# Decode layer with a mixture of experts: the last chunk's results are added in PSUM instead of stored, and the stored results are requested behind the last weights

## The chip, the cores and the metric

The kernel runs on one core of a Trainium2 chip. The metric is the device time of one execution in microseconds, the median of the runs.

## What is computed

One layer of a decoder for 256 prompt tokens and 32 sample tokens (8 sequences of 4), width 1024, in float32: a token mixer (sparse attention in three branches beside a gated linear recurrence), then a mixture of experts. Only the second half bears on the change:

```python
def moe_ffn(h, w_router, b_router, w_up, b_up, w_down, b_down):
    xt = h.reshape(-1, D)
    top_v, top_i = lax.top_k(xt @ w_router + b_router, TOP_K)      # 4 of 32 experts
    wts = jax.nn.softmax(top_v, axis=-1)
    gate_dense = sum over k of one_hot(top_i, 32) * wts            # token x expert
    for e in range(N_EXPERTS):
        z = xt @ w_up[e] + b_up[e]
        gate, up = min(z[:, :1024], 7), clip(z[:, 1024:], -7, 7)
        act = (up + 1.0) * gate * sigmoid(1.702 * gate)
        out = out + gate_dense[:, e:e + 1] * (act @ w_down[e] + b_down[e])
    return out
```

The layer's result is `x + gate * rms_norm(out)`, for the prompt and for the sample tokens.

## The kernel before

The five engines' programs are written out by hand in one block and meet in counted semaphores. `after(engine, name)` waits for a named step; the steps of TensorE, ScalarE and VectorE are counted in the order of the table `STEPS`. `link` makes an engine wait for its own last instruction.

**Order of the work.** Page gathers, modulation and input projection; attention of the sample tokens; then the prompt phase, in which `prompt_steps()` (a planner with costs in microseconds) lays out attention units (12 of them: two token tiles, three branches, two groups), the recurrence and the branch gates. The gates' weights come in 512 KB pieces into two buffers (`load_gate`, L621); SP asks for piece j once TensorE has used piece j-2 (`gate_ps`), and L1175 multiplies each in two halves. Semaphore `p_pv` counts finished attention units (L1099). Then the projections (L1254 to L1268), the router, and the routing: L2194 to L2234 on VectorE compute each token's row in its expert's chunks, the table `tab` (cumulated chunk counts per expert) and the weights `wts`.

**The expert loop.** The tokens of an expert are cut into chunks of 64 slots (`SLOT`). TensorE loops over experts and their chunks (34 chunks here). For a chunk it multiplies by 8 pieces of `w_up` (L1333), gathers the next chunk's tokens by a product with a 0/1 matrix (`dispatch`, L1304), transposes, and multiplies by 4 pieces of `w_down` into bank 4 (L1363). With 64 slots the two halves of the columns go to partitions 0 to 63 and 64 to 127 of a bank. Each piece of weights is 1 MB; SP issues them in order into a ring of 21 places (`load_piece`, L678), each when its place has been used (`piece_used`). ScalarE copies bank 4 to `yc` (L1715) and GpSimd stores `yc` with an indirect DMA (L2320) to `slots` in device memory, by token and choice, behind a small write (L2319); both count on `st_yc`. VectorE's `rowu` holds the rows.

**The tail.** Behind the weights SP waits for the last use by the last expert but one, then asks for `x` (`xl`, L707, L708), the experts' output bias `bdown` (L709) and the output gates (`gate_last`, L639, L640). Then it waits for `all_out`, which ScalarE gives when the last store has landed (L1718, L1719), and asks for the results of the 32 sample tokens (four loads, L714) and of the two prompt tiles (two loads of 2 MB, L716) into `gath`. TensorE transposes the token-by-expert weights `dense` (L1369; ScalarE copies them to `wT`), starts the sums of all three token tiles with the bias products (L1376), adds the sample rows' results by `wdiag` (L1380) and two of the four results of each prompt tile by `diag` (L1387). ScalarE and VectorE take the sample rows first (`ORDER` is 2, 0, 1): squares, root, `residual`; then `weighted(0)` and `weighted(1)` add the other two results (L2271, L2274), and two `residual` calls follow (L2154, L2156). SP stores y.

The ring, `xl`, `gate_last`, `bdown` and `gath` share one region: `gath` lies on ring places that the last expert still uses.

## Time and profile before

| | |
|---|---|
| median of 3 runs | 1582.41 us (1581.9 to 1583.75) |
| profiled execution | 1583.75 us, its span 1581.7 us |
| TensorE busy | 1450.6 us (92%) |
| VectorE, ScalarE, GpSimd busy | 367.3, 297.3, 81.6 us |
| granted TensorE clock | 0.965 of full speed in the mean |
| DMA | 513.21 MB, 324 GB/s in the mean |
| last request of the tail's first loads, first request of results | 1534.45 us, 1552.12 us |

The span runs from the first to the last instruction; times in the rows are microseconds from its start. An engine is called idle between its instructions, with what released it; a "form" is partitions by elements. The page cuts the span into 40 slices of 39.5 us.

### The profile page before, as it was taken

The page shows a single profiled execution, that of the slowest core. Times are in us where ns is not written, and L with a number is a line of the kernel's source. Part 1 is how long each engine was busy: PE and PEld are TensorE (multiplying, and loading weights), DVE is VectorE, ACT ScalarE, POOL GpSimd, SP SyncE. Part 2 cuts the span into 40 slices and gives each one's busy share as a digit, 9 for nine tenths or more (in the row PEclk, how much of TensorE's full clock was granted, in tenths as well). Part 3 has the DMA queues.
Part 4 walks back from the last instruction along what each step waited for, and adds up shares of the span by engine and source line. Part 5 has one row for each costly group of instructions (what it writes and reads, how often), then busy time and mean ns, then how long its engine had stood idle before and what let it go on. Part 6 is the DMA issues. An engine that isn't in the chain of part 4 may idle for free.

```text
span 1581.7 us, 21206 instructions
## 1 busy us (share of the span) xinstructions
PE 1450.6 (92%) x8595; PEld 649.6 (41%) x8595; DVE 367.3 (23%) x845; ACT 297.3 (19%) x568; POOL 81.6 (5%) x108
## 2 busy tenths in 40 slices
PE   4999989889998969999999999999998998899896
PEld 4554455378876543333333333333332222222221
DVE  5210012346852351111111111010101101110123
ACT  4100004544530221111111111111110110011011
POOL 2000002100000000000000000000000000000000
PEclk9999999978999969999999999999999999999997
DMA  9792774314269589979999999999999999999994
GB/s 276 245 321 80 290 257 171 84 42 140 60 164 292 213 327 383 416 310 417 418 414 417 417 415 416 419 416 415 417 417 417 415 417 417 414 418 416 415 404 175
DMA packets 136310, 513.21 MB, mean 324 GB/s; under 512 B 12945, under 2 KB 42025, under 8 KB 100962
## 3 DMA queue, kind: packets, MB, share of 16 engines
q1 hardware_dynamic: 129474, 489.91, 79.3%
q0 software_dynamic: 6752, 22.06, 4.1%
q8 instruction: 67, 1.10, 0.3%
q14 instruction: 17, 0.14, 0.0%
HBM read 501.06 MB, written 19.22 MB: 329 GB/s over the span
## 4 chain that ended last, share of the span: by engine, by line
PE 60%; DMA 29%; DVE 5%; SPq 3%; ACT 2%; issue 1%; POOL 0%; DVEq 0%; POOLq 0%; ACTq 0%
DMA arena<-in_w_up 23%; PE bank L1333 20%; PE bank L1363 9%; PE bank L1175 4%; PE bank L783 3%; PE bank L999 3%; PE bank L1000 3%; DMA arena<-in_w_in 2%; SPq L678 2%; PE bank L1268 2%; DMA arena<-in_cache_cmp,arena 2%; PE bank L1325 1%; PE bank L1254 1%; PE bank L1073 1%; PE bank L1256 1%
## 5 line engine op out<-in xcount | busy, mean ns | idle before, releaser
L1333 PE MATMUL bank<-arena 128*64 128x512 f32 x2176 | 498.0, 600 | 36.6 <-DMA arena<-in_w_up 36.3
L1333 PEld LDWEIGHTS bank<-arena 128*64 128x64 f32 x2176 | 145.0, 137 | 359.5 <-issue 262.0
L1363 PE MATMUL bank<-arena 128*64 128x512 f32 x1088 | 241.0, 595 | 0.0
L2245 DVE TENSOR_SCALAR arena<-bank,arena 128x1 uint32<-128x1 f32 x34 | 7.4, 219 | 597.7 <-PE bank L1341 580.4
L1363 PEld LDWEIGHTS bank<-arena 128*64 128x64 f32 x1088 | 75.0, 136 | 141.7 <-issue 135.7
L1708 ACT ACTIVATE arena<-arena 128x512 f32<-128x512 f32 x34 | 21.4, 630 | 536.3 <-DVE arena L2248 536.3
L1304 PE MATMUL bank<-arena 128*64 128x512 f32 (+1 forms) x420 | 103.0, 608 | 2.9 <-DVE arena L2206 2.9
L2319 POOL DMA_DIRECT2D slots<-arena x34 | 18.7, 551 | 1188.3 <-ACT arena L1715 1188.3
L1175 PE MATMUL bank<-arena 128*128 128x288 f32 x256 | 75.5, 445 | 2.4 <-DMA arena<-in_w_in 1.5
L2248 DVE TENSOR_SCALAR arena<-bank 128x512 f32<-128x512 f32 x34 | 23.5, 692 | 190.4 <-PE bank L1333 190.4
L999 PE MATMUL bank<-arena 128*128 128x512 f32 (+1 forms) x112 | 57.0, 590 | 8.4 <-DMA arena<-in_w_in 6.8
L1715 ACT COPY arena<-bank 128x512 f32<-128x512 f32 x34 | 19.9, 586 | 221.5 <-PE bank L1363 221.5
L1175 PEld LDWEIGHTS bank<-arena 128*128 128x128 f32 x256 | 51.3, 209 | 19.0 <-issue 2.8
L1304 PEld LDWEIGHTS bank<-arena 128*64 128x64 f32 (+1 forms) x420 | 26.9, 135 | 72.5 <-issue 69.4
L783 PE MATMUL bank<-arena 64*128 64x504 f32 x256 | 54.7, 584 | 1.7 <-DVE arena L1775 1.7
L1000 PE MATMUL bank<-arena 128*128 128x512 f32 (+1 forms) x112 | 55.9, 581 | 0.0
L1708 ACT ACT_TABLE_LOAD x34 | 43.6, 1283 | 0.6
L1325 PE MATMUL bank<-arena 32*64 32x512 f32 x272 | 37.9, 626 | 1.2 <-ACT arena L1699 1.2
L783 PEld LDWEIGHTS bank<-arena 64*128 64x128 f32 x256 | 25.1, 186 | 30.3 <-issue 30.3
L761 PE MATMUL bank<-arena 128*128 128x128 f32 x128 | 20.9, 325 | 17.1 <-DMA arena<-in_cache_cmp,arena 16.2
L2320 POOL DMA_INDIRECT slots<-arena x34 | 35.5, 1044 | 10.4 <-issue 10.4
L999 PEld LDWEIGHTS bank<-arena 128*128 128x128 f32 x112 | 21.5, 197 | 32.1 <-issue 22.4
(418 smaller groups left out, 1298.8 us busy)
## 6 DMA issues: line engine op xcount, KB each, us to landing
arena<-in_w_up SPq DMA_DIRECT2D x256, 1024.0 KB, 20.9
arena<-in_w_down SPq DMA_DIRECT2D x128, 1024.0 KB, 25.0
arena<-in_w_ada SPq DMA_DIRECT2D x12, 2048.0 KB, 11.8
arena<-in_w_in SPq DMA_DIRECT2D x6, 2048.0 KB, 13.2
arena<-in_w_in SPq DMA_DIRECT2D x16, 512.0 KB, 4.1
arena<-in_w_out SPq DMA_DIRECT2D x1, 4096.0 KB, 16.6
arena<-slots SPq DMA_DIRECT2D x2, 2048.0 KB, 10.3
out<-in_state_win SPq DMA_DIRECT2D x1, 4064.0 KB
```

Source lines behind the costliest of these rows:

```text
L678: sp.dma_start(dst, src).then_inc(S(f"ld_piece{n % R_}"), 16)
L783: last = mm(banks[2 * g + v][:, 0:NB * NCMP], w1[half, s], src, start=s == 0, stop=s == 31)
L999: mm(b0[:, 0:w], hT[:, k, 0:P], columns(k, 0, w), start=first, stop=final)
L1000: mm(b1[:, 0:w], hT[:, k, P:2 * P], columns(k, 0, w), start=first, stop=final)
L1175: last = mm(banks[7][:, 0:TP + NS], gate_piece[j % 2][:, k], hT[:, k], start=k == 0, stop=k == KD - 1)
L1268: last = mm(banks[(6, 2)[i] + n][:], mT[:, k, P * i:P * i + P], wo[k][:, 512 * n:512 * n + 512], start=k == 0, stop=k == KD - 1)
L1304: last = mm(banks[5][SLOT * s:SLOT * s + SLOT, :], oneslot[0:ROWS[i], i], h2r[0:ROWS[i], i, 512 * s:512 * s + 512], start=i == 0, stop=i == 2)
L1325: mm(banks[r // 2][SLOT * (r % 2):SLOT * (r % 2) + SLOT, :], ident[32 * r:32 * r + E, 32 * r + e:32 * r + e + 1].broadcast_to([E, SLOT]), ...
L1333: last = mm(banks[part][SLOT * s:SLOT * s + SLOT, :], xcT[:, q], ring[n % R_][:, D * part + 512 * s:D * part + 512 * s + 512], start=False ...
L1363: last = mm(banks[4][SLOT * s:SLOT * s + SLOT, :], lhs, ring[n % R_][:, D * v + 512 * s:D * v + 512 * s + 512], start=f == 0, stop=f == 7)
L1708: fn(sg, gt, ACT.Sigmoid, scale=1.702).then_inc(S("sig"), 1)
L2320: pool.indirect_dma_start(out=results, out_offset=bass.IndirectOffsetOnAxis(ap=rowu[:, 0:1], axis=0), in_=yc, in_offset=None, bounds_check ...
```

## The change

The last chunk is no longer stored. ScalarE still copies its result to `yc`; TensorE adds it to the three sums by products with `lastT`, a matrix slot by token that holds the token's weight where the token has that slot in the last chunk. So:

- GpSimd's loop runs over all chunks but the last. Rows of `slots` that the last chunk would have filled must be zero: early in the kernel GpSimd zeroes all of `slots` (4.72 MB, from a 128x128 tile of zeros, once the sixth attention unit is through) and waits for it.
- SP waits only for the stores of the chunks before the last (`st_yc` at `until * 32`) and asks for the results straight behind the gates.
- The output bias is loaded twice, to partitions 0 to 31 and 32 to 63, and the weights by expert are laid out twice (`dense2`), so that the two column halves of a bias product use different rows of the array. In the same way `lastT` holds the slots twice, beside the two halves of `yc`.
- VectorE computes the last chunk's first row (`last_row`), each token's weight in it (`last_k`, `last_sum`) and its slot (`slot0`) in the routing, builds `dense2` and `last_w` after its loop, and copies the transposed `lastT` out of bank 7 ahead of the diagonals.
- `gath` moves down by one ring place, to places that the last expert does not use.

```diff
@@ sync
-            sp.dma_start(bdown[0:E], A["b_down"][0]).then_inc(S("ld_bias"), 16)
+            for v in range(2):
+                sp.dma_start(bdown[E * v:E * v + E], A["b_down"][0]).then_inc(S("ld_bias"), 16)
             broadcast_rows(gate_last, 3 * D, "ld_gate")
-            after(sp, "all_out")
+            until = sp.value_load(tab[0:1, 3 * E - 1:3 * E], min_val=E - 1, max_val=CMAX - 1)
+            sp.wait_ge(S("st_yc"), until * 32)
@@ tensor
-            after(pe, "wdiag")
+            after(pe, "last_w")
             for i in range(3):
-                last = nc.tensor.transpose(banks[5][0:E, P * i:P * i + ROWS[i]], dense[0:ROWS[i], i], ident[0:ROWS[i], 0:ROWS[i]])
+                last = nc.tensor.transpose(banks[5][0:2 * E, P * i:P * i + ROWS[i]], dense2[0:ROWS[i], i], ident[0:ROWS[i], 0:ROWS[i]])
             last.then_inc(S("wT_ps"), 1)
+            for i in range(3):
+                last = nc.tensor.transpose(banks[7][:, P * i:P * i + ROWS[i]], last_w[0:ROWS[i], i], ident[0:ROWS[i], 0:ROWS[i]])
+            last.then_inc(S("lastT_ps"), 1)
             after(pe, "wT")
-            pe.wait_ge(S("ld_bias"), 80)
+            pe.wait_ge(S("ld_bias"), 96)
...
+            def down_bias(i):
                 for v in range(2):
+                    mm(banks[summed_in[i][v]][0:ROWS[i], :], wT[E * v:E * v + E, P * i:P * i + ROWS[i]],
+                       bdown[E * v:E * v + E, 512 * v:512 * v + 512], start=True, stop=False)
+
+            def last_rows(i):
+                for v in range(2):
+                    mm(banks[summed_in[i][v]][0:ROWS[i], :], lastT[SLOT * v:SLOT * v + SLOT, P * i:P * i + ROWS[i]],
+                       yc[SLOT * v:SLOT * v + SLOT, :], start=False, stop=False)
+
+            down_bias(0)
+            down_bias(1)
+            after(pe, "lastT")
+            down_bias(2)
+            after(pe, "yc_last")
+            for i in ORDER:
+                last_rows(i)
             pe.wait_ge(S("ld_gath2"), 64)
@@ scalar
-            act.wait_ge(S("st_yc"), n_chunks * 32)
-            nc.scalar.copy(gathered, eps_t).then_inc(S("all_out"), 1)
+            act.wait_ge(S("yc"), n_chunks)
+            nc.scalar.copy(gathered, eps_t).then_inc(S("yc_last"), 1)
@@ vector
+            V.memset(zero_t, 0.0).then_inc(S("zero_t"), 1)
...
             after(dve, "base_ps")
+            V.tensor_scalar(last_row, banks[3][:, 5 * E - 1:5 * E], float(SLOT), float(-SLOT), ALU.mult, ALU.add)
...
             V.tensor_scalar(wdiag, C("stack32"), wst, None, ALU.mult).then_inc(S("wdiag"), 1)
+            for i in range(3):
+                r = ROWS[i]
+                last = V.scalar_tensor_tensor(last_k[0:r, 4 * i:4 * i + 4], rowf[0:r, 4 * i:4 * i + 4], last_row[0:r], wts[0:r, i],
+                                              ALU.is_ge, ALU.mult)
+            link(dve, "dve", last)
+            for i in range(3):
+                last = V.tensor_reduce(last_sum[0:ROWS[i], i:i + 1], last_k[0:ROWS[i], 4 * i:4 * i + 4], AX, ALU.add)
+            link(dve, "dve", last)
+            until = dve.value_load(tab[0:1, 3 * E - 1:3 * E], min_val=E - 1, max_val=CMAX - 1)
+            V.tensor_copy(slot0, slot_of[:, :, bass.ds(until, 1)].rearrange("p i o -> p (i o)"))
+            link(dve, "dve", V.tensor_copy(ss[:, 3:4], eps_t))
...
+            for v in range(2):
+                V.tensor_copy(dense2[:, 0:2, E * v:E * v + E], dense[:, 0:2])
+                V.tensor_copy(dense2[0:NS, 2, E * v:E * v + E], dense[0:NS, 2])
+            for i in range(3):
+                for v in range(2):
+                    last = V.tensor_scalar(last_w[0:ROWS[i], i, SLOT * v:SLOT * v + SLOT], C("slot1")[0:ROWS[i]], slot0[0:ROWS[i], i:i + 1],
+                                           last_sum[0:ROWS[i], i:i + 1], ALU.is_equal, ALU.mult)
+            last.then_inc(S("last_w"), 1)
+            after(dve, "lastT_ps")
+            V.tensor_copy(lastT[:, 0:TP + NS], banks[7][:, 0:TP + NS]).then_inc(S("lastT"), 1)
@@ gpsimd
+            after(pool, "zero_t")
+            rows = slots[0:NRES].rearrange("(p a) (b c) -> p (a b) c", p=P, c=P)
+            pool.wait_ge(S("p_pv"), 6)
+            pool.dma_start(rows, zero_t.unsqueeze(1).broadcast_to([P, rows.shape[1], P])).then_inc(S("zero_slots"), 16)
+            pool.wait_ge(S("zero_slots"), 16)
             after(pool, "tab")
-            n_chunks = pool.value_load(tab[0:1, E - 1:E], min_val=E, max_val=CMAX)
-            with pool.Fori(0, n_chunks) as c:
+            until = pool.value_load(tab[0:1, 3 * E - 1:3 * E], min_val=E - 1, max_val=CMAX - 1)
+            with pool.Fori(0, until) as c:
```

## Rows read from the trace of the kernel before

**Rows 1.** The page: GB/s moved in each of 40 slices.
```profile
GB/s 276 245 321 80 290 257 171 84 42 140 60 164 292 213 327 383 416 310 417 418 414 417 417 415 416 419 416 415 417 417 417 415 417 417 414 418 416 415 404 175
```

**Rows 2.** Chain that ended last, the tail: start, length, what.
```profile
1547.33 0.59 ACT arena L1715
...
1549.44 2.44 DMA slots<-arena
...
1554.33 12.48 DMA arena<-slots
...
1566.86 3.71 PE bank L1387 x8
...
1572.04 1.28 DVE arena L2274
...
1577.41 1.23 DVE arena L2156
```

**Rows 3.** Windows: length, PE, PEld, DVE, ACT, POOL busy, PEclk, DMA share, GB/s.
```profile
1540.00:1545.00 5.00, 5.00 (x26) 1.75 (x26) 1.04 (x5) 0.59 (x1) 0.00 (x0) 1.00 0.77 264
1545.00:1550.00 5.00, 4.41 (x19) 1.51 (x16) 0.00 (x0) 0.87 (x2) 1.11 (x2) 0.98 0.15 55
1550.00:1555.00 5.00, 5.00 (x7) 1.35 (x6) 0.00 (x0) 0.19 (x1) 0.48 (x1) 0.50 0.42 127
1555.00:1560.00 5.00, 5.00 (x7) 0.71 (x5) 0.00 (x0) 0.00 (x0) 0.00 (x0) 0.50 1.00 376
1560.00:1565.00 5.00, 3.53 (x9) 1.44 (x8) 1.58 (x4) 2.83 (x6) 0.00 (x0) 0.99 1.00 429
```

**Rows 4.** Timeline of the tail: start, length, engine, line, form, idle before.
```profile
1544.89 0.14 PEld L1363 LDWEIGHTS bank<-arena 128*64 128x64 f32 x2 [0.29 <-DMA arena<-in_w_down]
...
1548.24 9.21 PE L1376 MATMUL bank<-arena 32*128 32x512 f32 x12 [0.59 <-ACT arena L1717]
...
1557.38 3.22 PE L1380 MATMUL bank<-arena 128*32 128x512 f32 x4
...
1560.64 0.59 ACT L1725 ACTIVATE arena<-bank 32x512 f32<-32x512 f32 x1 [8.55 <-PE bank L1380]
...
1563.53 0.15 DVE L2141 RECIPROCAL arena<-arena 32x1 f32<-32x1 f32 x1 [1.36 <-ACT arena L1668]
...
1566.29 1.39 DVE L2271 SCALAR_TENSOR_TENSOR arena<-arena,bank 128x512 f32<-128x512 f32 x2
```

**Rows 5.** SP's requests, and DMA issues of 1526 to 1536 (KB, us to landing).
```profile
1530.60 3.34 SPq L709 DMA_DIRECT2D arena<-in_b_down  x1
...
1534.45 0.76 SPq L640 DMA_DIRECT2D arena<-modd  x1
...
arena<-in_b_down SPq DMA_DIRECT2D x1, 128.0 KB, 17.2
arena<-modd SPq DMA_DIRECT2D x1, 128.0 KB, 14.9
```

**Rows 6.** The page's groups: count, busy us, mean ns, idle before.
```profile
L783 PE MATMUL bank<-arena 64*128 64x504 f32 x256 | 54.7, 584 | 1.7 <-DVE arena L1775 1.7
```

**Rows 7.** The prompt phase: TensorE's timeline, DMA issues of 385 to 395, windows.
```profile
386.12 1.00 PE L1099 MATMUL bank<-arena 128*128 128x64 f32 x8
...
394.61 2.86 PE L1175 MATMUL bank<-arena 128*128 128x288 f32 x8
...
408.05 2.21 PE L1175 MATMUL bank<-arena 128*128 128x288 f32 x8
...
arena<-in_w_in SPq DMA_DIRECT2D x1, 512.0 KB, 15.2
...
390.00:400.00 10.00, 10.00 (x47) 7.93 (x47) 9.14 (x22) 6.89 (x20) 0.00 (x0) 0.83 0.46 184
...
417.00:420.00 3.00, 3.00 (x29) 3.00 (x29) 2.93 (x8) 1.78 (x3) 0.00 (x0) 1.00 0.66 175
```

**Rows 8.** VectorE's timeline, first work of its chunk loop.
```profile
602.67 0.22 DVE L2245 TENSOR_SCALAR arena<-bank,arena 128x1 uint32<-128x1 f32 x1 [6.30 <-PE bank L1341]
```

29 lines of the change are left out of this document (16 added, 13 removed).

## The prediction

> **What bounds the kernel now.** I began with the page's line of bytes per slice [rows 1]. From the nineteenth slice on the DMA engines move 414 to 419 GB/s (404 in the next to last): the expert weights stream at one rate for some 800 us, so work of the expert loop is paid only if it holds that stream back. The last slice shows 175 GB/s: the weights are through and something else sets the end. So the chain that ended last was read next, for the tail only [rows 2]. From the last chunk's result to the end it runs: ScalarE empties bank 4 at 1547.33 (L1715), GpSimd stores the chunk and the store takes 2.44 us to land from 1549.44, SP then issues six loads, the second big load of `slots` lands 12.48 us after 1554.33, TensorE adds its share (3.71 us from 1566.86), and VectorE works to 1578.64 (1577.41 + 1.23). Between there and the span's 1581.7 lies the store of y, 3.06 us.
>
> The windows of that stretch [rows 3] show what is wasted. In 1545 to 1550 the core moves 55 GB/s and in 1550 to 1555 127 GB/s, while nothing but the fetch of results is left to do. The tail waits for bytes that could not be asked for before the last store had landed. The second fact in these windows is the clock: 0.98, 0.50, 0.50, 0.99. TensorE fell to its lower level (1.2 of 2.4 GHz) at about 1549.9, while it ran the bias products of L1376, and came back at about 1560.
>
> The timeline gives the prices [rows 4]. One 128x512 fp32 product shows as two instructions: L1387's eight instructions (four products) take 3.71 us at full clock [rows 2], so one costs some 0.86 us in a longer run. L1376's six products took 9.21 us and L1380's two 3.22, at the lower level. VectorE is nearly back to back once it starts: first reciprocal 1563.53, first weighted sum 1566.29, so the sample rows cost 2.76; a weighted sum costs 2.70 (1.39, 1.28 and the gap); from the end of the second one (1572.04 + 1.28 = 1573.32) to that of the chain [rows 2] are 5.32 for two residuals. ScalarE starts on the sample rows at 1560.64 and VectorE follows 2.89 later.
>
> **Part 1, the loads move forward.** SP's last requests of before end at 1535.21 [rows 5]. The last of them lands 14.9 us after 1534.45, at 1549.35, and the bias 17.2 after 1530.60, at 1547.8: the requests sit in the queue behind the last weights. After the change SP waits only for the next to last chunk's store, which GpSimd issued a chunk earlier (some 30 us), so SP walks through, and the copy of the bias and the results' six loads are asked for from about 1535 to 1539. They land behind 1549.35. Their bytes are 0.13 + 0.52 + 2.10 + 2.10 MB; the fetch ran at 429 GB/s in 1560 to 1565 [rows 3]. That gives the second bias copy about 1548.1 (0.3 behind the first), the sample rows 1550.9, the first prompt tile 1555.8, the second 1560.7. In the kernel before the second landed at 1566.81 (1554.33 + 12.48). I take the slowest DMA engine for this: those that are done early (share 0.77 in 1540 to 1545) only help.
>
> Does this traffic slow the last weights? TensorE took the last `w_down` piece with the same 0.29 us gap as between any two weight loads [rows 4], so there is no slack. Between 0 and +1 us (a gain is excluded: nothing ahead of them is taken away); I take 0, since the requests stand behind the weights in the same queue and the stream shows one rate with all engines busy.
>
> The Trainium skill ("DMA: Bandwidth & Descriptors", Queues, rings and completion order) says that descriptors of one queue start in ring order on each engine. By it this cost is zero too; no row here shows two requests of one queue overtaking, and the sum above does without it.
>
> **Part 2, the last store goes.** It frees 1547.92 to 1552.1 on the chain. ScalarE now signals `yc_last` right behind its copy of the 64 rows of wT, at about 1548.5. No cost.
>
> **Part 3, new products.** TensorE transposes wT (now 64 columns) and then three more tiles: short ones, beside ScalarE's copy of bank 4. VectorE then copies 128x288 out of PSUM ahead of the diagonals, no more than the 0.59 us of ScalarE's 128x512 copy [rows 2]. The bias products of tiles 0 and 1 start when they did, at 1548.24, and cover that copy. Bias products now come in pairs on two 32-row strips and the last chunk's in pairs on two 64-row strips. Pairs of this sort exist in the kernel: L783, on 64 rows, shows 256 instructions in 54.7 us busy [rows 6], 0.214 us each, so a pair (four instructions) costs 0.86 us, what one product alone costs. Three bias pairs: 2.6 us instead of 9.21. Three last-chunk pairs: 2.6 us new. Two sample products: 1.7 us. Sum at full clock: 1548.24 + 2.6 + 2.6 + 1.7 = 1555.2 for the point where ScalarE starts on the sample rows; 1560.64 before.
>
> The clock is the unknown. Low end: it never falls, 1555.2. High end: it falls at 1549.9 as before and stays low for all that is left up to that point, four pairs and two products, 5.15 us at full: 1560.3. I take half of the pairs at the lower level (the last bias pair and one of the last chunk's, +1.7): the bias pairs resemble L1376, under which it fell, the 64-row pairs use all rows of the array as the loop does, whose clock is 1.00 [rows 3]. So 1556.9.
>
> From there: VectorE starts 2.89 later, 1559.8; sample rows 2.76, 1562.6; first weighted sum 1565.3 (its products end 3.7 us after 1556.9, its data came at 1555.8); second weighted sum: TensorE has data at 1560.7 and needs 3.7, so 1564.4, no wait; 1568.0; residuals 5.32, 1573.3; store 3.06: 1576.4. Against 1581.7 this is **-5.3 us**. VectorE's chain is now what is late. With the full clock the second sum waits for its data (1564.4): end 1575.5, -6.2. With the high end 1579.8, -1.9.
>
> **Part 4, zeroing `slots`.** GpSimd writes 4.72 MB of zeros in 512-byte rows once the sixth attention unit is through, at 387.1 [rows 7]. No such transfer is in the trace. Nearest rows: a gate piece, 0.52 MB in rows of 512 bytes, uses 0.66 of 3 us, so 2.0 us of all engines; nine times that is 18 us of DMA time. The engines have room: 46% is used in 390 to 400, then a piece of 2 us in every 9 or so. Who could suffer: the piece that SP asked for at 386.3, behind the 4 MB copy of the window state. It landed 15.2 us later, at 401.5, and TensorE wants it at 408.05 (L1175, the first half two gates on; the 394.61 group is the gate between). Slack 6.5 us; sharing its 2 us with the fill costs 2 to 4 us. Cost 0; bound above: the piece waits for all of the fill, 401.5 + 18 = 419.5, a stall of 11.4 us. A gain is excluded. GpSimd's wait for the fill holds up nothing: its next work is the first chunk's store.
>
> The Trainium skill ("DMA: Bandwidth & Descriptors", Issuing engines are not separate DMA queues) says that transfers started from different engines run on the same 16 DMA engines and interleave. It speaks against the fill: a private queue of GpSimd gives no cover. With interleaving the piece makes its time; the bound above is what a strict order would give.
>
> **Part 5, small VectorE work.** One 128x1 operation stands ahead of `slotb`, on the path that restarts the weights: the like of it is 0.22 us with the next starting 0.13 later [rows 8], so +0.15. The seven operations and the register load behind `wdiag`, some 2 to 3 us, end inside the 6.30 us that VectorE waited at 602.67. The memset at the start and the copies and six small operations after the loop (about 2 us beside 7 us of products) cost nothing.
>
> **Rivals.**
> (a) The clock stays low until about 1560, as before: the arithmetic above, -1.9 + 0.15. For it: it fell under narrow products, and six transposes stand ahead of them. Against: the new pairs fill more of the array. 1580.7 us.
> (b) **Slower:** the fill holds up the gates. TensorE is busy 10.00 of 10 us in 390 to 400 [rows 7] and nearly so to 440, so a stall there goes to the end. Up to 6.5 us of delay of the piece are free, the next 5.2 eat the gain; beyond 11.7 us the kernel is slower. With the whole fill ahead: 11.4 of stall, net +6.3, 1588.7 us. Against: 5 us of free DMA time in 390 to 400 alone, and the rest of the piece's own time is only 2 us.
> (c) The low clock lasts through the diagonals too. Then the second prompt tile's sum is ready at about 1574, end 1585, +3.5: 1586 us. Against: in the kernel before it rose under L1380, narrower than the products here.
> (d) The change does not do what it says: SP's requests are held back by a full queue (the bias request took 3.34 us [rows 5]) or by the wait. Up to 1549 a late request costs little, since the slowest engine is not free before. If they start only at 1552, the second prompt tile lands at 1566.8 as before and the same chain follows it: no gain, 1582.5 us. Against: the earlier chunk's store has had ten times the 2.44 us that the last one took [rows 2].
>
> **How the numbers follow.** The profiled execution took 1583.75 us, 1.34 above the median 1582.41, with a span of 1581.7. I apply the difference to the median: 1582.41 - 5.3 + 0.15 = **1577.3 us**. Chances: the forecast with its clock range (-3.5 to -6.5) 0.70; (a) 0.10; (d) 0.05; (b) in part, a few us of stall, 0.07, and whole 0.03; (c) 0.02; the last weights slowed 0.03. The range: full clock without the wait for the second tile below (-6.9, and 0.7 for the spread of runs), (a) and a little of (b) above; it leaves out (c), (d) and the whole of (b): 1574.8 to 1581.4. A measurement here can tell about 0.2% (3.2 us) from no change. Faster by more than that (under 1579.2): 0.74. Within: 0.18. Slower: 0.08.
>
> **What would show it.** Right: requests of `slots` from about 1536, no fall of the GB/s between 1540 and 1560; the bias products in about 2.6 to 3.5 us; the sample rows on ScalarE at 1555 to 1558.5; VectorE with no idle time from its first reciprocal to the end. Wrong: PEclk 0.50 up to 1560 (a, c); a wait of L1175 for `w_in` between 390 and 440, or L1254 starting later than 491 (b); `slots` landing after 1563 (d); L1363 waiting for `w_down` near 1545.

## The result and the profile after

The change made the kernel slower. The median of nine runs is 1594.16 us (1586.6 to 1597.66) against 1582.41 before; the ratio is 1.0074 with a 95% interval of 1.006 to 1.0087. The profiled execution took 1594.34 us with a span of 1592.4, 10.7 over the span of before. The forecast was 1577.3 us, with a chance of 0.08 for slower.

Two places show it at once. The first is the prompt phase, read as [rows 7] was. The chain that ended last, the page's DMA issues, TensorE's timeline at the gate products (L1184, L1175 before), and the windows (length, PE, PEld, DVE, ACT, POOL busy, PEclk, DMA share, GB/s):

```profile
385.97 27.10 DMA arena<-in_w_in
...
slots<-arena POOLq DMA_DIRECT2D x1, 4608.0 KB, 26.8
...
413.11 3.83 PE L1184 MATMUL bank<-arena 128*128 128x288 f32 x8 [4.98 <-DMA arena<-in_w_in]
...
390.00:400.00 10.00, 9.71 (x44) 7.73 (x44) 9.04 (x23) 7.26 (x21) 0.46 (x1) 0.83 0.94 331
400.00:410.00 10.00, 7.81 (x47) 5.98 (x45) 8.05 (x17) 7.15 (x18) 0.00 (x0) 0.98 0.96 302
410.00:420.00 10.00, 6.89 (x30) 5.68 (x31) 3.76 (x7) 2.08 (x8) 0.00 (x0) 0.68 0.25 80
```

The piece of `w_in` asked for at 385.97 landed 27.1 us later, 15.2 before. TensorE waited 4.98 us for it and went on at a lower clock (0.68 in the last window). The fill itself took 26.8 us, and with it the DMA engines were full for some 20 us (share 0.94 and 0.96).

The second place is the tail. TensorE's timeline, and the windows of the same stretch, which answer to [rows 3, 4]:

```profile
1546.98 5.37 PE L1372 MATMUL bank<-arena 128*64 128x512 f32 x24
1554.75 1.94 PE L1372 MATMUL bank<-arena 128*64 128x512 f32 x8 [2.40 <-DMA arena<-in_w_down]
...
1560.76 5.63 PE L1389 MATMUL bank<-arena 32*128 32x512 f32 x12 [3.04 <-DMA arena<-in_b_down]
1566.32 4.79 PE L1394 MATMUL bank<-arena 64*32 64x512 f32 x12
1571.04 1.91 PE L1406 MATMUL bank<-arena 128*32 128x512 f32 x4
```

```profile
1545.00:1550.00 5.00, 4.81 (x26) 1.90 (x24) 3.27 (x14) 1.18 (x2) 0.00 (x0) 1.00 1.04 291
1550.00:1555.00 5.00, 2.60 (x14) 0.78 (x12) 0.00 (x0) 0.00 (x0) 0.00 (x0) 1.00 1.04 229
1555.00:1560.00 5.00, 2.72 (x14) 0.87 (x10) 1.24 (x5) 0.96 (x3) 0.00 (x0) 0.99 1.06 261
1560.00:1565.00 5.00, 4.24 (x10) 1.45 (x12) 0.00 (x0) 0.00 (x0) 0.00 (x0) 0.50 0.96 302
1565.00:1570.00 5.00, 5.00 (x12) 1.02 (x10) 0.00 (x0) 0.00 (x0) 0.00 (x0) 0.50 0.63 269
```

The idle gap of before (55 and 127 GB/s in [rows 3]) is indeed filled, but not at 429 GB/s: the DMA engines are full (share 1.04) and move 229 to 302. The last `w_down` piece comes 2.40 us late, the bias another 3.04, and the clock is at its lower level for all the new products. The page's issues show the rest: the results of the prompt tiles, 10.3 us from request to landing before, now take 26.2 (median of the two).

```profile
arena<-slots SPq DMA_DIRECT2D x2, 2048.0 KB, 26.2
```

The difference of the two spans, stage by stage:

| from | to | before | after | difference |
|---|---|---|---|---|
| start | first expert weights asked for | 525.95 | 532.21 | +6.3 |
| first weights | last chunk's down products begin | 1014.2 | 1014.8 | +0.6 |
| that | end of the last chunk | 7.0 | 9.6 | +2.6 |
| end of the last chunk | ScalarE begins on the sample rows | 13.5 | 16.4 | +2.9 |
| sample rows | end of the span | 21.1 | 19.4 | -1.6 |

The table compares one execution of each kernel. In its first row that is safe: the two traces lie within 0.1 us of each other up to the wait (TensorE starts the group at 408.05 before, and is ready for it at 408.1 after), and part behind it. The last row is the change's gain, and it came as forecast: VectorE no longer waits between its first reciprocal and the end. Everything ahead of it got longer.

### The profile page after: what moved, and what is told of

The parts are those of the page before. It is cut to its first block, busy times and chain, and to the rows that moved or that the text cites. A ratio compares the mean times of both kernels' runs of the same rounds, so it can differ in the third digit from the quotient of the medians.

```text
span 1592.4 us, 21261 instructions
## 1 busy us (share of the span) xinstructions
PE 1451.6 (91%) x8610; PEld 652.5 (41%) x8610; DVE 371.5 (23%) x866; ACT 297.0 (19%) x568; POOL 83.0 (5%) x107
## 4 chain that ended last, share of the span: by engine, by line
PE 58%; DMA 30%; DVE 5%; SPq 3%; ACT 2%; issue 1%; POOL 0%; DVEq 0%
DMA arena<-in_w_up 22%; PE bank L1342 19%; PE bank L1372 8%; DMA arena<-in_w_in 4%; PE bank L1184 4%; PE bank L792 4%; PE bank L1008 3%; PE bank L1009 2%; SPq L684 2%; PE bank L1277 2%; DMA arena<-in_cache_cmp,arena 2%; PE bank L1334 1%; DMA arena<-in_b_down 1%; PE bank L1263 1%; PE bank L1265 1%
## 5 line engine op out<-in xcount | busy, mean ns | idle before, releaser
L1372 PE MATMUL bank<-arena 128*64 128x512 f32 x1088 | 241.2, 595 | 2.4 <-DMA arena<-in_w_down 2.4
L1372 PEld LDWEIGHTS bank<-arena 128*64 128x64 f32 x1088 | 75.0, 136 | 144.3 <-issue 135.4
L1184 PE MATMUL bank<-arena 128*128 128x288 f32 x256 | 75.1, 443 | 7.1 <-DMA arena<-in_w_in 6.3
L1184 PEld LDWEIGHTS bank<-arena 128*128 128x128 f32 x256 | 51.1, 209 | 23.7 <-DMA arena<-in_w_in 7.7
L792 PEld LDWEIGHTS bank<-arena 64*128 64x128 f32 x256 | 28.5, 195 | 29.8 <-issue 29.8
L2376 POOL DMA_INDIRECT slots<-arena x33 | 34.7, 1051 | 10.4 <-issue 10.4
## 6 DMA issues: line engine op xcount, KB each, us to landing
arena<-in_w_ada SPq DMA_DIRECT2D x12, 2048.0 KB, 11.7
slots<-arena POOLq DMA_DIRECT2D x1, 4608.0 KB, 26.8
arena<-slots SPq DMA_DIRECT2D x2, 2048.0 KB, 26.2
```

What stands on the lines that cost most here:

```text
L792: last = mm(banks[2 * g + v][:, 0:NB * NCMP], w1[half, s], src, start=s == 0, stop=s == 31)
L1184: last = mm(banks[7][:, 0:TP + NS], gate_piece[j % 2][:, k], hT[:, k], start=k == 0, stop=k == KD - 1)
L1372: last = mm(banks[4][SLOT * s:SLOT * s + SLOT, :], lhs, ring[n % R_][:, D * v + 512 * s:D * v + 512 * s + 512], start=f == 0, stop=f == 7)
L2376: pool.indirect_dma_start(out=results, out_offset=bass.IndirectOffsetOnAxis(ap=rowu[:, 0:1], axis=0), in_=yc, in_offset=None, bounds_check ...
```

## Experiments

Every kernel was timed beside new runs of the kernel before on the same chip, so each ratio stands on its own. The time at which the weights start differs between executions by up to 9.5 us even between kernels that don't differ up to there (first weights request 517.3 in e10, 526.8 in e11), so traces are compared stage by stage and times by ratios. Each trace is one execution.

| kernel | ratio to before | 95% interval | last chunk's down products | end of last chunk to sample rows | sample rows to end |
|---|---|---|---|---|---|
| before | | | 7.0 | 13.5 | 21.1 |
| after | 1.0074 | 1.006 to 1.0087 | 9.6 | 16.4 | 19.4 |
| e1_fill_only | 1.0071 | 1.0044 to 1.0097 | 7.0 | 12.8 | 22.7 |
| e8_before_fill_early | 0.9994 | 0.9975 to 1.0012 | 7.0 | 12.8 | 23.4 |
| e3_fill_early | 1.0021 | 1.0005 to 1.0037 | 9.5 | 16.8 | 19.4 |
| e4_late_requests | 0.999 | 0.9973 to 1.0007 | 7.2 | 15.5 | 19.4 |
| e5_sample_rows_early | 1.0027 | 1.001 to 1.0044 | 8.9 | 16.6 | 19.4 |
| e6_bias_first | 0.9997 | 0.9982 to 1.0013 | 8.3 | 9.9 | 22.4 |
| e7_sample_first | 1.0007 | 0.999 to 1.0024 | 7.7 | 12.4 | 22.6 |
| e9_x_behind_results | 0.9965 | 0.9949 to 0.9982 | 7.0 | 8.9 | 19.4 |
| e10_one_sample_load | 1.0005 | 0.9989 to 1.0021 | 7.0 | 14.0 | 21.6 |
| e11_no_late_wait | 1.0005 | 0.9986 to 1.0025 | 13.5 | 8.9 | 19.4 |
| e12_one_load_alone | 0.9991 | 0.9972 to 1.0009 | 7.0 | 8.9 | 24.2 |
| e13_four_loads_alone | 0.997 | 0.9949 to 0.999 | 7.0 | 8.9 | 20.8 |

### e1_fill_only: the fill alone, at its place

The kernel before, with nothing of the change but the fill (and the zeros it copies):

```diff
+            after(pool, "zero_t")
+            rows = slots[0:NRES].rearrange("(p a) (b c) -> p (a b) c", p=P, c=P)
+            pool.wait_ge(S("p_pv"), 6)
+            pool.dma_start(rows, zero_t.unsqueeze(1).broadcast_to([P, rows.shape[1], P])).then_inc(S("zero_slots"), 16)
+            pool.wait_ge(S("zero_slots"), 16)
```

> The kernel before with the zeroing of slots alone added, at its place after the sixth attention unit. Theory A (the fill holds up a gate piece): the piece asked for at about 386 lands some 27 us later instead of 15.2, L1175 waits about 5 us for in_w_in near 408 and starts at the lower clock, the first weights request moves from 525.9 to about 532, and the kernel is 6 us slower, about 1588.5 us. Rival (the fill is hidden and the loss of the changed kernel lies in its tail alone): 1582.4 us, no wait near 408.

Measured: 1590.52 us, ratio 1.0071. TensorE's timeline and the page's issues show the wait of the changed kernel again:

```profile
409.29 3.80 PE L1175 MATMUL bank<-arena 128*128 128x288 f32 x8 [5.00 <-DMA arena<-in_w_in]
...
slots<-arena POOLq DMA_DIRECT2D x1, 4608.0 KB, 26.7
```

By the ratio the fill alone costs as much as the whole change (11 us, within 7 to 15). The rival of a hidden fill is out. The trace accounts for less of it: 5.0 us of wait and 1.6 more in the group behind it; the first weights request came at 528.5, not at 532. Where the other 4 us of the ratio lie no run shows. The old tail in this trace:

```profile
1551.18 6.08 PE L1376 MATMUL bank<-arena 32*128 32x512 f32 x12 [0.59 <-ACT arena L1717]
1559.18 3.62 PE L1380 MATMUL bank<-arena 128*32 128x512 f32 x4 [1.91 <-DMA arena<-slots]
```

The bias products take 6.08 us here where they took 9.21 in the trace of before [rows 4]: the clock fell only at about 1556, in their last microsecond, and TensorE then waited for `slots` instead.

### e3_fill_early and e8_before_fill_early: the fill some 90 us earlier

e3 is the changed kernel without GpSimd's wait for the sixth attention unit, so the fill is asked for at about 297; e8 is e1 with the same edit.

```diff
-            pool.wait_ge(S("p_pv"), 6)
```

> The changed kernel with the zeroing started right behind the last page gathers (about 297 us) instead of after the sixth attention unit. Theory A: the prompt phase is that of the kernel before again (first weights request at about 526), which takes 6 us off, to about 1588 us; what is left, some 5 us over before, is the tail, where the last w_down piece and the second copy of the bias land late. Rival (the tail goes as predicted and only the fill costs): 1577 us.

> The kernel before with the fill of the result rows alone added, but asked for some 90 us earlier than the change does (as in e3_fill_early), beside the selected rows' work and not beside the gate's weights. Theory: the fill costs only by the load that it delays; here nothing urgent is on the way, and the time is that of before (ratio 1.000, at most 1.001), against 1.0071 for the same fill at the place of the change. The tail's part of the change is then what e3 and e4 show against this kernel. Rival: 4.7 MB of writes cost wherever they are, since all of the prompt phase is near the bandwidth; then the ratio is 1.003 or more and the tail's part of the change is a gain hidden under it.

Measured: e3 1584.44 us, ratio 1.0021; e8 1581.74 us, ratio 0.9994. In the kernel before nothing moves at that time; in e8 the fill has it. The windows of 306 to 316, first of before, then of e8:

```profile
306.00:316.00 10.00, 5.09 (x28) 1.95 (x24) 4.30 (x13) 5.96 (x11) 0.00 (x0) 0.91 0.00 0
```

```profile
306.00:316.00 10.00, 4.18 (x24) 1.73 (x20) 5.17 (x15) 5.43 (x9) 0.00 (x0) 0.91 0.99 271
```

The gate's wait for `in_w_in` is gone in both. So the same 4.7 MB cost 0.7% (11 us) at one place and nothing that can be measured at the other. The rival of e8 (a cost wherever the fill stands) is out. What is left in e3 is the tail's own: 1.0021 against 0.9994 is a loss of 4 us (the intervals touch, so none to 8), where a gain of 5 was forecast. TensorE's timeline of e3 has the two waits of the changed kernel, nothing of the fill being near:

```profile
1543.73 1.94 PE L1372 MATMUL bank<-arena 128*64 128x512 f32 x8 [2.22 <-DMA arena<-in_w_down]
...
1550.09 5.63 PE L1389 MATMUL bank<-arena 32*128 32x512 f32 x12 [3.39 <-DMA arena<-in_b_down]
1555.65 4.88 PE L1394 MATMUL bank<-arena 64*32 64x512 f32 x12
```

### e4_late_requests and e5_sample_rows_early: do requests behind the weights slow them?

In e4 SP waits for the landing of the last `w_down` piece before it asks for any result; in e5 the same wait stands behind the sample tile's four loads (0.5 MB) and ahead of the prompt tiles' two only.

```diff
             sp.wait_ge(S("st_yc"), until * 32)
+            sp.wait_ge(S(f"ld_piece{(PIECES - 1) % R_}"), 16 * ((PIECES - 1) // R_) + 16)
             by_token = slots[0:NRES].rearrange("(t k) d -> t k d", k=TOPK)
```

> As e3_fill_early, and SP asks for the results in slots only once the last piece of w_down has landed (about 1545 us). Theory B (the early requests slow the last weights and the bias, both still in flight): L1372 no longer waits for w_down, the bias is there when TensorE is, the results land from about 1548 to 1560 and the kernel takes about 1578 us. Rival C (the second bias copy or the new products are what costs): as slow as e3_fill_early, about 1587 us.

> As e3_fill_early, but only the four 128 KB loads of the sample rows (32 partitions each) are asked for behind the gates; the two loads of 2 MB wait until the last piece of w_down has landed. Theory B1 (the loads on 32 partitions slow the packets of all engines): the last w_down piece and the second bias copy are as late as in e3_fill_early, about 1586 us. Theory B2 (the bytes of the large loads do it): w_down and the bias are in time and the kernel takes about 1578 us.

Measured: e4 1579.91 us, ratio 0.999, against 1.0021 for e3 on the same chip; e5 1584.45 us, ratio 1.0027. TensorE's timeline of e4 (two lines) and of e5 (one):

```profile
1539.65 7.22 PE L1373 MATMUL bank<-arena 128*64 128x512 f32 x32
...
1549.93 5.63 PE L1390 MATMUL bank<-arena 32*128 32x512 f32 x12 [2.04 <-DMA arena<-in_b_down]
```

```profile
1542.74 1.94 PE L1373 MATMUL bank<-arena 128*64 128x512 f32 x8 [1.64 <-DMA arena<-in_w_down]
```

In e4 TensorE does not wait for `in_w_down`; in e5 it waits 1.64, and the intervals of the two ratios lie apart. So the requests that stand behind the last weights in one queue do slow them, and the 0.5 MB of the sample tile are enough. Theory B missed on the bias, which was not in time. It still came 2.04 us late in e4, 2.89 in e5, and the products ran at half clock in both (5.63 and 4.97 us in e4).

### e6_bias_first: the bias asked for ahead of x

```diff
+            for v in range(2):
+                sp.dma_start(bdown[E * v:E * v + E], A["b_down"][0]).then_inc(S("ld_bias"), 16)
             sp.dma_start(xl[:, 0:2], xd[0:TP].rearrange("(i p) d -> p i d", p=P)).then_inc(S("ld_x"), 16)
             sp.dma_start(xl[0:NS, 2], xd[TP:TP + NS]).then_inc(S("ld_x"), 16)
-            for v in range(2):
-                sp.dma_start(bdown[E * v:E * v + E], A["b_down"][0]).then_inc(S("ld_bias"), 16)
```

> The kernel of e4_late_requests (fill early, results requested behind the landing of the last down weights), with the two copies of the down bias requested ahead of the rows of x instead of behind them. Theory: the bias products of e4 started 2.04 us late only because the bias copies stand behind 1 MB of x rows in the queue; they now land 2 to 3 us earlier, the wait is gone, and from the end of the last chunk's down products to ScalarE's sample rows it takes 13.5 us instead of 15.5; the time falls by about 2 us against e4, ratio to before about 0.998. Rival: the copies are late because all loads behind the weights are slow on their 32 partitions, in whatever order; the wait stays over 1 us and the time stays at e4's 0.999. Second rival: with the wait gone TensorE stays at its full clock and the bias and last-chunk products take 5.2 us instead of 10.6; then ratio about 0.994.

Measured: 1579.74 us, ratio 0.9997. TensorE's timeline:

```profile
1550.41 2.96 PE L1390 MATMUL bank<-arena 32*128 32x512 f32 x12
1553.30 2.97 PE L1395 MATMUL bank<-arena 64*32 64x512 f32 x12
1557.23 1.90 PE L1407 MATMUL bank<-arena 128*32 128x512 f32 x4 [0.96 <-DMA arena<-slots]
1561.97 3.67 PE L1414 MATMUL bank<-arena 128*128 128x512 f32 x8 [2.83 <-DMA arena<-slots]
1566.78 3.70 PE L1414 MATMUL bank<-arena 128*128 128x512 f32 x8 [1.13 <-DMA arena<-slots]
```

The wait for the bias is gone, and with no wait ahead of them the products ran at full clock: 2.96 and 2.97 us against 5.63 and 4.97. The second rival was right on the clock, and wrong on the time: what was gained on TensorE turned into waits for the results. The last of them came 17.5 us behind the end of the last chunk, 19.7 in the kernel before. The time is that of e4 within the intervals. Now the landing of the results is late, not TensorE. TensorE also waited 1.04 us for the last `w_down`, with the results' requests held back (0.46 in e7, none in e4): 2.1 MB of other loads stand behind the weights in all three, 0.5 MB in e9 below, where there is no such wait.

### e7_sample_first: is it TensorE or the landing?

e6 with TensorE's tail in another order: the sample tile's bias, last-chunk and weighted products, then all of one prompt tile, then all of the other.

```diff
-            down_bias(0)
-            down_bias(1)
             after(pe, "lastT")
             down_bias(2)
             after(pe, "yc_last")
-            for i in ORDER:
-                last_rows(i)
+            last_rows(2)
...
+                down_bias(i)
+                last_rows(i)
                 pe.wait_ge(S(f"ld_gath{i}"), 16)
```

> The kernel of e6_bias_first, with TensorE's order in the tail changed: bias, last-chunk and weighted products of the sample tile first, then all of the first prompt tile, then all of the second. Theory: at half clock the 12.5 us of products ahead of ScalarE's sample rows were the whole loss; only 5.4 us of them stay ahead, so the sample rows start about 7 us earlier than in e6, but the prompt tiles' products (some 14 us at half clock behind the sample's) then bind VectorE: TensorE ends 20 to 21 us behind the last chunk and the time falls by 1 us against e6 at half clock, up to 4.6 us if the clock comes back by the diagonal products. Rival: TensorE is not what binds and only the landing of the results is (4 MB behind the last down weights, last piece some 15 us behind its request); then the sample rows are early, the prompt tiles wait for their results, and the time is e6's.

Measured: 1583.32 us, ratio 1.0007. TensorE was ready 5 us before the sample tile's results were, and its clock fell while it waited:

```profile
1550.94 1.05 PE L1395 MATMUL bank<-arena 64*32 64x512 f32 x4
1557.00 3.58 PE L1404 MATMUL bank<-arena 128*32 128x512 f32 x4 [5.00 <-DMA arena<-slots]
```

The theory is refuted in its main point (sample rows 7 us earlier than in e6: they came 2.5 us later, measured from the end of the chunk). The rival holds in that the landing binds, though the sample rows weren't early.

### e9_x_behind_results: 1.5 MB moved behind the results

The prompt tiles' rows of x and their gate row are needed only by VectorE's last two steps. They were asked for ahead of the results; here behind them.

```diff
-            sp.dma_start(xl[:, 0:2], xd[0:TP].rearrange("(i p) d -> p i d", p=P)).then_inc(S("ld_x"), 16)
             sp.dma_start(xl[0:NS, 2], xd[TP:TP + NS]).then_inc(S("ld_x"), 16)
-            broadcast_rows(gate_last, 3 * D, "ld_gate")
+            sp.dma_start(gate_last[0:NS, 1], modd[1:1 + NS, 3 * D:4 * D]).then_inc(S("ld_gate"), 16)
...
                 sp.dma_start(gath[:, 4 * i:4 * i + 4], by_token[P * i:P * i + P]).then_inc(S(f"ld_gath{i}"), 16)
+            sp.dma_start(xl[:, 0:2], xd[0:TP].rearrange("(i p) d -> p i d", p=P)).then_inc(S("ld_s0"), 16)
+            sp.dma_start(gate_last[:, 0], modd[0:1, 3 * D:4 * D].broadcast_to([P, D])).then_inc(S("ld_s0"), 16)
```

> The kernel of e6_bias_first, with the two loads that nothing needs before VectorE's last two steps (the prompt tiles' rows of x, 1 MB, and their gate row spread over 128 partitions, 0.5 MB) requested behind the results of the prompt tiles instead of ahead of them. Theory: in e6 the landing of the results binds (TensorE waited 0.96, 2.83 and 1.13 us for them); with 1.5 MB less ahead of them they land 3.5 to 5 us earlier, the waits go, VectorE runs through from the sample rows on (19.4 us to the end as in e4) and the sample rows start 1 to 2 us earlier: about 3 us under e6, ratio to before 0.9975 to 0.998. Rival: the slow part is the loads on 32 partitions, which all stay ahead; then the results land at most 2 us earlier and the time is within 1 us of e6's.

Measured: 1574.67 us, ratio 0.9965 with 0.9949 to 0.9982, faster than both kernels; span 1572.0. TensorE's timeline, and windows:

```profile
1536.70 7.09 PE L1374 MATMUL bank<-arena 128*64 128x512 f32 x32
1543.72 0.55 PE L1380 MATMUL bank<-arena 128*64 128x128 f32 x3
1544.21 0.61 PE L1383 MATMUL bank<-arena 128*128 128x128 f32 x3
1544.84 2.96 PE L1391 MATMUL bank<-arena 32*128 32x512 f32 x12
1547.73 2.97 PE L1396 MATMUL bank<-arena 64*32 64x512 f32 x12
1550.63 1.91 PE L1408 MATMUL bank<-arena 128*32 128x512 f32 x4
1552.47 7.36 PE L1415 MATMUL bank<-arena 128*128 128x512 f32 x16
```

```profile
1545.00:1550.00 5.00, 5.00 (x22) 1.49 (x24) 1.09 (x5) 0.00 (x0) 0.00 (x0) 1.00 0.99 410
1550.00:1555.00 5.00, 5.00 (x14) 1.61 (x11) 0.15 (x1) 2.41 (x5) 0.00 (x0) 1.00 0.96 408
```

No wait is left in the tail, on TensorE or, from its first reciprocal on, on VectorE, the clock is full, and the results come at 410 GB/s, 10.4 us behind their requests. From the start of the last chunk's down products to the end it takes 35.3 us against 41.6 before. The theory holds, with a gain of 5 us on e6 where it gave 3.

### e10_one_sample_load and e12_one_load_alone: one request for the sample tile

```diff
-            for k in range(TOPK):
-                sp.dma_start(gath[NS * k:NS * k + NS, 8], by_token[TP:TP + NS, k]).then_inc(S("ld_gath2"), 16)
+            sp.dma_start(gath[:, 8], by_token[TP:TP + NS].rearrange("t k d -> k t d")).then_inc(S("ld_gath2"), 16)
```

e12 adds a wait for its landing ahead of the prompt tiles' requests.

> The kernel of e9_x_behind_results, with the sample tile's results loaded by one request over 128 partitions instead of four requests of 32 partitions each, same bytes and same places. Theory that loads on 32 partitions take longer packets: the 0.5 MB move faster, their landing and that of the prompt tiles' results comes 1 to 2 us earlier than in e9, and GB/s of the stretch behind the weights rises above 300. Rival: bytes and order alone count; then the landings are e9's, and the time within 0.1% of it.

> The kernel of e10_one_sample_load (the sample tile's results by one request over 128 partitions), with SP waiting until they have landed before it requests the prompt tiles' results. In e10 the sample rows landed 17 us and the prompt tiles' results 19 to 23 us behind their requests, with the DMA engines full at 229 to 241 GB/s. Theory (two loads of different shape at the same time slow each other): alone the sample rows land in 3 to 4 us, the tiles' results in 5 to 8 us more at over 400 GB/s, and the time is e9's (ratio 0.996 to 0.998). Rival (the single request is slow in itself): it takes over 8 us to land alone, TensorE waits 3 us or more for slots ahead of the sample products, and the time is no better than e10's 1.0005.

Measured: e10 1582.31 us, ratio 1.0005; e12 1579.62 us, ratio 0.9991. The one request over 128 partitions was slower, not faster. In e10 the prompt tiles' results landed 19.2 us behind their requests (10.4 in e9). In e12 the load ran alone, and SP's next request shows that it took 8.1 us to land; TensorE had it in time, and waited 4.44 us for the prompt tiles' results instead. The windows of e10 first, then SP's timeline, a line of TensorE's and the windows of e12:

```profile
1540.00:1545.00 5.00, 4.98 (x23) 1.59 (x23) 1.24 (x5) 0.43 (x3) 0.00 (x0) 1.00 1.08 229
1545.00:1550.00 5.00, 1.63 (x7) 0.37 (x4) 0.00 (x0) 0.00 (x0) 0.00 (x0) 0.87 0.93 241
```

```profile
1540.63 0.70 SPq L722 DMA_DIRECT2D arena<-slots  x1
...
1548.78 0.85 SPq L725 DMA_DIRECT2D arena<-slots  x2
...
1556.63 8.65 PE L1415 MATMUL bank<-arena 128*128 128x512 f32 x16 [4.44 <-DMA arena<-slots]
...
1540.00:1545.00 5.00, 4.98 (x26) 1.75 (x22) 0.49 (x2) 0.96 (x3) 0.00 (x0) 1.00 0.17 53
1545.00:1550.00 5.00, 5.00 (x24) 1.35 (x20) 0.75 (x4) 0.00 (x0) 0.00 (x0) 1.00 0.36 99
```

With this load alone under way (1543 to 1548) 23 to 26% of the 16 engines' time is used, at 94 to 100 GB/s: as much as four of them have. The Trainium skill ("DMA: Bandwidth & Descriptors", Why a DMA increments its semaphore by 16 and not by 1) states that a transfer is spread over the largest number of engines up to 16 that divides the slowest dimension of both its patterns; here that is the source's k, with 4. The share in this trace agrees. So the rival of e12 holds on the load (slow in itself) and on the time, which does not differ from e10's by more than the intervals; the wait came at another place than it said, and e10 did not test the partitions at all: it put one slow load in the place of four quick ones. It shows something else, though. While this load and the tiles' ran together, the engines were full and moved 229 to 241 GB/s, as in the changed kernel.

### e11_no_late_wait and e13_four_loads_alone: what e9 owes to its wait

e11 is e9 without SP's wait for the last `w_down`; e13 is e9 with one more wait, for the sample tile's four loads, ahead of the prompt tiles' requests.

```diff
-            sp.wait_ge(S(f"ld_piece{(PIECES - 1) % R_}"), 16 * ((PIECES - 1) // R_) + 16)
```

```diff
+            sp.wait_ge(S("ld_gath2"), 64)
             for i in range(2):
                 sp.dma_start(gath[:, 4 * i:4 * i + 4], by_token[P * i:P * i + P]).then_inc(S(f"ld_gath{i}"), 16)
```

> The kernel of e9_x_behind_results without SP's wait for the last down weights ahead of the requests for the results (as the change has it). Theory: requests that stand behind the last weights in the queue still slow them, because the 16 DMA engines do not come to the end of the weights together; TensorE waits 1.5 to 2.5 us for in_w_down at the end of the last chunk as in e3, the results themselves land earlier by 1 to 2 us, and the time is 0 to 2 us over e9's. Rival: the weights' lateness comes from elsewhere (e6 and e7 have 0.5 to 2 us of it with the wait); then e11 is 1 to 2 us faster than e9 by its earlier results.

> The kernel of e9_x_behind_results, with the same wait: the prompt tiles' results are requested only when the sample tile's four loads have landed. Theory (loads of different shape slow each other while they overlap): the four loads land in 2 to 3 us as in e9, the tiles' results then move at 426 GB/s from the start and land at most 1 us later than in e9, where their first 3 us moved at 250 GB/s; TensorE waits for none and the time is e9's within 0.1%. Rival: the wait costs its full round of 2 to 4 us ahead of the tiles, TensorE waits for them, and the time is 1 to 3 us over e9's.

Measured: e11 1582.06 us, ratio 1.0005; e13 1575.57 us, ratio 0.997. TensorE's timeline and the windows of e11:

```profile
1545.81 1.94 PE L1373 MATMUL bank<-arena 128*64 128x512 f32 x8 [0.96 <-DMA arena<-in_w_down]
1551.11 3.63 PE L1373 MATMUL bank<-arena 128*64 128x512 f32 x8 [3.37 <-DMA arena<-in_w_down]
...
1545.00:1550.00 5.00, 1.94 (x8) 0.49 (x8) 0.00 (x0) 0.00 (x0) 0.00 (x0) 1.00 1.07 202
1550.00:1555.00 5.00, 3.89 (x10) 0.91 (x10) 0.00 (x0) 0.13 (x1) 0.00 (x0) 0.66 0.94 208
```

The wait alone is worth 0.4%, 6 us. Without it the last chunk's down products take 13.5 us instead of 7.0, and behind them the tail is e9's to a tenth. The mechanism was expected; its size (0 to 2 us) was not. In e13 TensorE waited 1.08 and 1.16 us for the results, where the theory had no wait. The time is e9's within the intervals, but they are too wide to tell it from the rival's 1 to 3 us more: from the start of the last chunk's down products to the end e13's trace has 36.6 us, 1.4 more than e9's.

## Why the prediction was wrong

The direction was wrong. Two steps failed most: part 4 put the fill's cost at 0 (measured: a wait of 5.0 us and 1.6 us at a lower clock, 11 us by e1's ratio), and part 1 let the results land at 429 GB/s at no cost to the last weights (measured: full engines at 229 to 302 GB/s, and weights and bias 2.4 and 3.0 us late). Taken by its own steps:

**What bounds the kernel.** Right. The gap between the last weight and the results was waste, and e9 shows that most of it can be had: the results are asked for 2.7 us ahead of the last chunk's end (5.0 behind it before), and the gain is near what the full-clock case of the sum gives (-6.2 us; measured -0.35%, 5.5 us). A shorter gap is left (41 GB/s in 1541 to 1542).

**Part 1, the loads move forward: the landing times failed.** SP did ask early (at 1543.93, right behind its requests for the gate rows, with the last chunk's down products still to come). But the sum let the results land one after the other at 429 GB/s, a rate read from [rows 3] where nothing but the two big loads was under way, and took 0 for the last weights. Measured: 229 to 302 GB/s with full engines over some 18 us, the last of the sample rows' four loads 19.8 us (13.1 in the median) and the prompt results 26.2 us behind their requests, the last weights 2.4 us late (e3: 2.2; e11: 4.3; with the requests held back none in e4 and e9, 1.04 in e6, 0.46 in e7). The 0.03 for "last weights slowed" stood on the order within the queue. The order held, and did not help. The last landings in after are in order: `w_down` about 1554.7, the second bias copy 1560.7, the last sample rows 1565.2, the tiles 1569.9 and 1574.7. What failed is "those that are done early (share 0.77 in 1540 to 1545) only help": the 16 engines don't come to the end of the weights together, and while those that are ahead run later requests, the others are slower. The packet records of the traces (start, length, size and queue of each packet) show it. In e9, with no request for results behind the weights, the packets of 4 KB that are under way thin out from 13 at 1535 to 1 at 1541, when the last `w_down` has landed, and a packet takes 0.16 us to the end. In e11 the first 16 KB packets of the prompt tiles' results start at 1537.6, while `w_down` is still on its way to others; from 1543 to 1551 a packet of 4 KB takes 0.36 us and one of 16 KB 1.26 us (medians), where alone they take 0.16 and 0.61. That the rows of before show "no two requests overtaking" says nothing of how fast the engines are while both are in them. The second bias copy, forecast for 1548.1, 1.0 us behind the end of the last chunk, was 3 to 4 us too late in after and e3, since it stood behind 1.2 MB of x (in e6, ahead of it, it was in time).

**Part 2, the last store.** Right: gone, no cost.

**Part 3, the new products: the clock term was mis-sized.** The counts and the full-clock prices were right within 15%: three bias pairs 2.96 us, three last-chunk pairs 2.97, sample products 1.91 in e9, against 2.6, 2.6 and 1.7. With +1.7 us for the clock the step from the end of the last chunk to the sample rows was to be 9.8 us. It was 16.4: 3 for the bias, and half clock for all pairs. Rival (a) had the clock but not its cause. In before it fell under busy, narrow products, and I looked for it there; in after, e3, e4, e5 and e7 it was down behind a wait of 2 to 5 us for a load, and in e6 and e9, with no wait ahead of these products, it stayed at 1.00. Over all traces of the tail it came down during each of the eight waits of 2.89 to 5.00 us (after, e3, e5, e7, e8, e10, e11, e12). Of five waits of 2.04 to 2.83 us it came down with two (2.04 in e4, 2.71 in e1) and not with three (2.22 in e3, 2.40 in after, 2.83 in e6). So in these runs a late transfer was paid twice, but what brings the clock down is argued from which cases go together, and not shown: in before, e1 and e8 it fell within the old bias products, with no wait over 0.59 us ahead of them. There is a second fault in the base. The 9.21 us of the old bias products are half-clock time of one execution (6.08 in e1, 6.05 in e8), and lay under the fetch, since L1387 still had to wait for `slots` behind them; shortening them was no gain in itself: e1 and e8 have them short, and take 35.4 and 36.2 us from the end of the last chunk to the end, before 34.6.

**From the sample rows on.** Right: 19.5 us forecast, 19.4 measured.

**Part 4, the fill: the step that cost most.** Its own size was about right (18 us of DMA time forecast; alone in e8 it ran at 271 GB/s, and landed after 22.6 us). Wrong was "sharing its 2 us with the fill costs 2 to 4 us". The piece was delayed by 11.9 us, 27.1 against 15.2, and the packet records show how:

| | before | after |
|---|---|---|
| last packet of the 4 MB copy ahead of the piece ends | 399.5 | 398.9 |
| first 512 of the piece's 1024 packets (512 bytes each) | 387.6 to 390.4 | 387.9 to 390.2 |
| other 512 packets | 398.1 to 401.0 | 398.7 to 413 |
| of these per us | some 175 | 40 |
| fill packets (4096 bytes) per us, on all engines | none | 75 to 78 |

The copy was not held up by the fill. In both kernels one half of the piece runs at once and the other only when the copy ends; the difference is the second half's own 2.9 against 14.3 us, 11.4 of the 11.9. From 409 on the other engines are through with the fill, and 39 to 42 of its packets per us are left beside 34 to 43 of the piece's. The records carry no engine number, but by these counts the two take turns packet by packet, and the fill's are eight times as large. e1 shows the same (41 per us from 395), and in e3 and e8, where the fill is over by then, the second half runs as before. I counted bytes where packets are served, and gave the fill only the engines' free time. That time was misread too: the copy alone kept 7.5 packets under way on average, so the 46% in use were about half of the engines full and the other half free, not room on each. With 11.9 us of delay and a slack of 6.5 the sum would have given 5.4 of stall; measured are 5.0 of wait, 1.6 more in the group behind it (3.83 against 2.21) at a lower clock, and 6.3 at the first weights. Rival (b), slower, had the right mechanism and place, and too small a chance. It also called 11.7 us of delay the point from which the kernel gets slower, which holds only with the tail's gain behind it. The Trainium skill ("DMA: Bandwidth & Descriptors", Issuing engines are not separate DMA queues) says that transfers of different issuing engines interleave on the same DMA engines. The trace agrees, packet for packet as above; "with interleaving the piece makes its time" was my own step, and it was wrong.

**Part 5.** Not contradicted: +0.6 us over the 1014 us of the expert loop, where 0.15 was forecast ahead of it; neither can be told apart from the spread.

**The signs named.** Bias products at 5.63 instead of 2.6 to 3.5; the sample rows at 1572.98 instead of 1555 to 1558.5, of which 9.5 us are the later end of the last chunk; `slots` landing at 1574.7 instead of by 1563, though SP's requests were not held back as rival (d) had it; L1372's wait for `w_down`, L1184's for `w_in`, and PEclk 0.50: each of the signs given for wrong is there.

What stays open is why packets take twice as long in these stretches (229 to 302 GB/s in after, 229 to 241 in e10, 202 and 208 in e11, with full engines). 256 packets of 16 KB bring the prompt tiles' results; 5 to 7% of them take over 0.9 us in before, e9, e12 and e13, and 34, 42 and 43% in after, e10 and e11. Two sizes side by side are not enough for it: in e11 from 1556 to 1564 packets of 4 KB and 16 KB run together at 0.16 and 0.61 us. Eight of the ten loads of the tail that stand ahead of the prompt tiles' results in after go to 32 partitions. The Trainium skill ("SBUF — State Buffer", Door 1: The DMA port swizzle) states that partitions 0 to 63 reach only 8 of 16 ports, with 196 GB/s measured for them against 328 for all 128, at 1 MiB. The 202 and 208 GB/s of e11 are near that figure, but e10's stretch of 229 to 241 had a load over 128 partitions in it, so the runs do not settle it. Open too are what brings the clock down, and the 4 us of e1's ratio that its trace doesn't show.

## What to carry to other kernels

A transfer that is put beside others is not paid from the engines' free share: a share of 46% was half of the engines full. Ask which load under way has the least slack (what stands ahead of it in its queue uses that up) and how small its packets are next to the new transfer's, since they take turns packet by packet; and move the new transfer to a stretch where no load is urgent. Behind a stream that must come in time, ask for the next loads in the order in which they are needed, and only when the stream has landed; earlier requests in the same queue run on the engines that are done first, and slow the rest. And take a rate from a stretch with the same mix of loads, not from the best one in the trace.

## What was not expected of the hardware

- 16 full DMA engines moved 202 to 241 GB/s (e10, e11) and 229 to 302 (after) with mixed loads in one queue, 408 to 429 with large loads alone.
- A fill of 4.7 MB, moved in packets of 4096 bytes, delayed a load of 0.5 MB in packets of 512 bytes by 11.9 us, though 54% of the engines' time had been free in that stretch: 40 packets per us of each on the engines they shared (after), some 175 of the load's alone (before).
- The engines came to the end of the weights and of the small loads behind them up to 6 us apart (e9, 1535 to 1541), and packets of later requests on the early ones go with packets of twice the length on the late ones (e11, 0.36 against 0.16 us).
- One request with a slowest dimension of 4 took 8.1 us for 0.5 MB (e12); four requests of 32 rows had all landed 4.4 us behind the first of them (e13).
- TensorE's granted clock came down during each of eight waits of 2.89 to 5.00 us for a load, and the same products took 5.63 instead of 2.96 us (after, e9); of five waits of 2.04 to 2.83 us three left it up.
